# Three feed-forwards of a two-block network, cut by quarters, with 512-column matmuls over both parts of the activation

## The reference

```
u = rms_norm(h, norm_mlp[l])                                       # (256, 1024)
h = h + jnp.square(jax.nn.relu(u @ w_up[l])) @ w_down[l]           # w_up (1024, 4096), w_down (4096, 1024)
```

## Time and profile before

| | |
|---|---|
| median of 3 runs | 1058.03 us (1057.1 to 1058.78) |
| span of the profiled execution, first to last instruction | 1055.0 us |
| mean granted TensorE clock | 0.998 |
| busy: PE, PEld, DVE, ACT, POOL | 98%, 96%, 68%, 51%, 3% |
| moved by DMA | 167.01 MB, mean 158 GB/s |

### The profile page before, as it was taken

One profiled execution on the slowest core, in us unless ns is written; L12 is line 12 of the kernel. 1 busy time (PEld: TensorE's weight loads), 2 busy tenths in 40 slices (PEclk: granted clock), 3 DMA queues, 4 the chain that ended last, 5 costly groups with the idle time before them and its releaser, 6 DMA issues.

```text
span 1055.0 us, 21161 instructions
## 1 busy us (share of the span) xinstructions
PE 1038.3 (98%) x8984; PEld 1008.7 (96%) x8984; DVE 715.8 (68%) x1007; ACT 536.1 (51%) x639; POOL 32.6 (3%) x39
## 2 busy tenths in 40 slices
PE   7999999999999999999999999999999999999997
PEld 7999999999997899999999999999898999999997
DVE  6989665455567787666565567899978666555454
ACT  7847553434446464355445346897543255443431
POOL 0004000000000000000000000042000000000000
PEclk9999999999999999999999999999999999999999
DMA  9722475546744646565555553424100257555511
GB/s 293 222 81 82 160 262 177 194 166 203 275 157 141 219 160 204 159 186 211 186 172 184 182 191 120 140 73 152 58 2 2 64 179 253 183 189 171 196 40 40
DMA packets 119057, 167.01 MB, mean 158 GB/s; under 512 B 5840, under 2 KB 99664, under 8 KB 118608
## 3 DMA queue, kind: packets, MB, share of 16 engines
q1 hardware_dynamic: 117808, 165.92, 47.9%
q10 hardware_dynamic: 1184, 0.17, 0.1%
HBM read 165.03 MB, written 1.05 MB: 157 GB/s over the span
## 4 chain that ended last, share of the span: by engine, by line
PE 84%; DVE 10%; ACT 2%; issue 2%; SPq 1%; DMA 1%; DVEq 0%; ACTq 0%
PE banks L2084 25%; PE banks L2086 25%; PE banks L2085 24%; DVE sb_w_low L1237 2%; DVE sb_arena L1917 1%; DVE sb_state L1914 1%; DMA sb_raw<-in_w_in 1%; PE banks L2668 1%; PE banks L2535 1%; SPq L539 1%; PE banks L2779 0%; DVE sb_arena L1405 0%; DVE sb_state L1402 0%; PE banks L2838 0%; PE banks L2822 0%
## 5 line engine op out<-in xcount | busy, mean ns | idle before, releaser
L1237 DVE TENSOR_TENSOR sb_w_low<-sb_raw,sb_w_high 128x2048 fp32r<-128x2048 f32 x148 | 338.0, 2289 | 242.1 <-ACT sb_w_high L660 242.0
L660 ACT ACTIVATE sb_w_high<-sb_raw 128x2048 fp32r<-128x2048 f32 x148 | 281.8, 1911 | 262.9 <-PE banks L2086 261.7
L2084 PE MATMUL banks<-sb_act_high,sb_w_low 128*128 128x256 f32 x1352 | 386.3, 286 | 1.1 <-DVE sb_arena L1790 0.7
L2086 PE MATMUL banks<-sb_act_high,sb_w_high 128*128 128x256 f32 x1352 | 381.9, 282 | 0.0
L2085 PE MATMUL banks<-sb_act_low,sb_w_high 128*128 128x256 f32 x1352 | 380.0, 281 | 0.0
L2084 PEld LDWEIGHTS banks<-sb_act_high,sb_w_low 128*128 128x128 f32 x1352 | 254.6, 188 | 3.3 <-DVE sb_arena L1790 0.9
L2085 PEld LDWEIGHTS banks<-sb_act_low,sb_w_high 128*128 128x128 f32 x1352 | 255.9, 189 | 0.5 <-issue 0.2
L2084 PE MATMUL banks<-sb_hidden_high,sb_w_low 128*128 128x256 f32 x896 | 253.6, 283 | 0.0
L2086 PEld LDWEIGHTS banks<-sb_act_high,sb_w_high 128*128 128x128 f32 x1352 | 253.4, 187 | 0.0
L2086 PE MATMUL banks<-sb_hidden_high,sb_w_high 128*128 128x256 f32 x896 | 253.4, 283 | 0.0
L2085 PE MATMUL banks<-sb_hidden_low,sb_w_high 128*128 128x256 f32 x896 | 251.9, 281 | 0.0
(11 more groups left out here) (443 smaller groups left out, 1048.6 us busy)
## 6 DMA issues: line engine op xcount, KB each, us to landing
sb_raw<-in_ffn_w SPq DMA_DIRECT2D x64, 1024.0 KB, 5.2
sb_raw<-in_w_up SPq DMA_DIRECT2D x16, 1024.0 KB, 5.4
sb_raw<-in_w_down SPq DMA_DIRECT2D x16, 1024.0 KB, 5.0
sb_raw<-in_sgu_w_in SPq DMA_DIRECT2D x16, 1024.0 KB, 5.3
sb_raw<-in_rwkv_w_rkv SPq DMA_DIRECT2D x12, 1024.0 KB, 5.2
sb_raw<-in_w_in SPq DMA_DIRECT2D x8, 1024.0 KB, 9.6
sb_raw<-in_sgu_w_out SPq DMA_DIRECT2D x8, 1024.0 KB, 4.9
sb_raw<-in_w_out SPq DMA_DIRECT2D x4, 1024.0 KB, 5.1
```

Source lines behind the costliest of these rows:

```text
L660: nc.scalar.activation(whi[s][:], raw[s][:], ACT.Copy).then_inc(hi_done, 1)
L1237: nc.vector.tensor_tensor(wlo[s][:], raw[s][:], f32(whi[s][:]), ALU.subtract).then_inc(lo_done, 1)
L2084: nc.tensor.matmul(dst, l_lo, r_hi, start=start, stop=False, **kw)
L2086: return nc.tensor.matmul(dst, l_hi, r_hi, start=False, stop=stop, **kw)
```

## The change

The feed-forward goes in four quarters of 1024 hidden channels. A quarter is four up units and then four down units, and a down unit now multiplies the quarter's 1024 hidden channels with 256 output channels (`inner` loads, not `outer`). `FFN_ORDER` lists the 32 units. High and low part of an activation tile lie in one buffer, so that one moving operand of 2 x 256 columns has both. `wide` issues two matmuls in place of three: the high weights times both parts, 512 columns over a whole bank, and the low weights times the high part, 256 columns into the bank's second half. The two halves of a bank have to be added, which `add_half` does for the two tiles of a unit by one `tensor_reduce` on DVE, of 2 x 256 x 2 values. Units go round three pairs of banks; PE waits before unit m until unit m-3 is taken. An up unit is then relu-squared by one scalar_tensor_tensor on DVE (max with 0, times itself), copied to the high part by ACT, subtracted by DVE. A down unit is scaled and added to `x` at once, a quarter of the sum at a time. The first two down units of a quarter are interleaved: 6 of 8 k tiles of each, then the last 2 of each. The last unit of a feed-forward uses `split_matmul` as before and is taken by tiles. All loops are unrolled. The low parts of the next stage come after the last full unit has been taken.

```diff
+    act_parts = place("act_parts", 0, [P, 2, KT, T], F32R)
+    act_hi, act_lo = act_parts[:, 0], act_parts[:, 1]
...
+    FFN_ORDER = []
+    for _q in range(4):
+        FFN_ORDER += [("up", i) for i in range(4 * _q, 4 * _q + 4)]
+        FFN_ORDER += [("down", _q, n) for n in range(4)]
+    FFN_BANK = lambda m: 2 * (m % 3)
+    halves_at = lambda b: banks[:, 512 * b:512 * b + 1024].rearrange("p (t h n) -> p t h n", t=2, h=2)
...
 (ACT, mlp)
+            for m in range(len(FFN_ORDER) - 1):
+                if m + 4 < len(FFN_ORDER) or (m + 4 < len(FFN_ORDER) + 2 and u0 + m + 4 < n_units):
+                    high(u0 + m + 4)
+                if FFN_ORDER[m][0] == "up":
+                    hidden_high(m)
...
 (DVE, mlp)
+            def add_half(m, t):
+                dve.wait_ge(w_used, u0 + m + 1)
+                nc.vector.tensor_reduce(t, halves_at(FFN_BANK(m)).rearrange("p t h n -> p t n h"), AX_X, ALU.add)\
+                    .then_inc(unit_taken, 1)
+                dve.wait_ge(unit_taken, 31 * j + m + 1)
+            def up_taken(m):
+                if FFN_ORDER[m][1] or j:
+                    dve.wait_ge(h_sq, 16 * j + FFN_ORDER[m][1])
+                add_half(m, FB.r)
+                nc.vector.scalar_tensor_tensor(FB.h, FB.r, 0.0, FB.r, ALU.max, ALU.mult).then_inc(h_sq, 1)
+            def hidden_low(m):
+                i = FFN_ORDER[m][1]
+                slot = FB.slots[i % 4]
+                dve.wait_ge(h_hi, h0 + i + 1)
+                nc.vector.tensor_tensor(slot[:, 1], FB.h, f32(slot[:, 0]), ALU.subtract).then_inc(h_lo, 1)
+            def down_taken(m):
+                q, n = FFN_ORDER[m][1:]
+                d = down_before(m)
+                t = FB.t[j][d % 2]
+                if d == 14:
+                    dve.wait_ge(x_done, FFN_XO[j] + 1)
+                elif d >= 2:
+                    dve.wait_ge(x_added, 12 * j + min(d - 1, 12))
+                add_half(m, t)
+                chain.add(nc.vector.tensor_tensor(t, t, over(FB.r2[j], 2), ALU.mult))
+                if q:
+                    dve.wait_ge(x_added, 12 * j + 4 * (q - 1) + n + 1)
+                chain.settle()
+                xs = x[:, 2 * n:2 * n + 2, :]
+                nc.vector.tensor_tensor(xs, xs, t, ALU.add).then_inc(x_done if q == 3 else x_added, 1)
+            for m in range(len(FFN_ORDER) - 1):
+                if FFN_ORDER[m][0] == "up":
+                    up_taken(m)
+                else:
+                    down_taken(m)
+                u = u0 + m + 3
+                if m and (m + 3 < len(FFN_ORDER) or (m + 3 < len(FFN_ORDER) + 2 and u < n_units)):
+                    low(u)
+                if FFN_ORDER[m][0] == "up":
+                    hidden_low(m)
+                if m == 3:
+                    token_scale()
...
+            for c in range(3):
+                after_sum(c)
+            t, b = FB.t[j][1], FFN_BANK(len(FFN_ORDER) - 1)
...
+            for i in range(2):
+                if i:
+                    dve.wait_ge(w_used, u0 + len(FFN_ORDER))
+                else:
+                    dve.wait_ge(last_tile, j + 1)
+                chain.add(nc.vector.tensor_tensor(t[:, i, :], tiles_at(b)[:, i, :], FB.r2[j], ALU.mult))
                 chain.settle()
+                nc.vector.tensor_tensor(x[:, 6 + i, :], x[:, 6 + i, :], t[:, i, :], ALU.add)\
+                    .then_inc(x_done if i else x_tile, 1)
+            after_sum(3)
...
 (PE, mlp)
+            def wide(dst, l_hi, l_lo, parts, start, stop):
+                nc.tensor.matmul(two(dst), l_hi, parts, start=start, stop=False, skip_group_check=True)
+                return nc.tensor.matmul(dst[:, T:2 * T], l_lo, parts[:, 0, :], start=False, stop=stop,
+                                        skip_group_check=True)
+            def begin(m):
+                q = (u0 + m) % RING
+                pe.wait_ge(lo_done, u0 + m + 1)
+                if m >= 3:
+                    pe.wait_ge(unit_taken, 31 * j + m - 2)
+                return (w[q][:, :].rearrange("p (k n) -> p k n", k=KT) for w in (whi, wlo))
...
+            for m0 in range(0, len(FFN_ORDER), 8):
+                for m in range(m0, m0 + 4):
+                    up(m)
+                if m0 == 0:
                     pe.wait_ge(sq_folded, j + 1)
                     nc.tensor.matmul(bank[6][:, 0:T], ones, FB.ss[j], start=True, stop=True).then_inc(ss_done, 1)
+                down(m0 + 4, range(6))
+                down(m0 + 5, range(6))
+                down(m0 + 4, range(6, KT))
+                down(m0 + 5, range(6, KT))
+                down(m0 + 6)
+                if m0 + 7 < len(FFN_ORDER) - 1:
+                    down(m0 + 7)
+                else:
+                    down_last(m0 + 7)
```

More of the change, by code:

```diff
@@ L499, in mlp @@
                 sp.wait_ge(tail_ps, ps_at(3, "Y"))
[L500 to L517, removed]
+            for m in range(2, len(FFN_ORDER)):
+                if m == 6 and j == 1 and on["rwkv"]:
+                    load_lora_first()
+                if m == len(FFN_ORDER) - 2:
+                    after_loop()
+                kind, *at = FFN_ORDER[m]
+                if kind == "up":
+                    inner(u0 + m, up, at[0])
+                else:
+                    q, n = at
+                    inner(u0 + m, down[:, 8 * q:8 * q + 8, :], n)
         def load_sgu():
@@ L857, in mlp @@
             high(u0 + 3)
[L859 to L900, removed]
-                        n = i - 2
-                        act.wait_ge(la_scaled, n + 1)
-                        nc.scalar.activation(la_hi[n][:], RW.la_sc[n], ACT.Copy).then_inc(la_hi_done, 1)
-            else:
-                with act.Fori(1, FCH - 2) as i:
-                    body(i)
@@ L1565, in body, with token_scale @@
-            def body(i, last):
-                hidden(i)
-                low(u0 + 6, i)
-                low(u0 + 7, i)
-                if not last:
-                    low(u0 + 8, i)
-                    low(u0 + 9, i)
-            if j == 1 and on["rwkv"]:
-                for i in range(FCH - 2):
-                    body(i, False)
-                    if i in (1, 2):
-                        scale_lora(i - 1)
-                    elif i in (3, 4):
-                        n = i - 3
+            def token_scale():
+                dve.wait_ge(ss_done, SS[("ffn1", "ffn2", "ffn3")[j]] + 1)
+                chain.add(nc.vector.tensor_scalar(FB.r2[j], bank[6][:, 0:T], 1.0 / D, EPS, ALU.mult, ALU.add))
+                chain.settle()
+                chain.add(nc.vector.reciprocal(FB.r2[j], FB.r2[j]))
@@ L1592, in mlp @@
-            chain.settle()
-            for c in range(4 if j < 2 else 3):
-                accumulated(FFN_ACC[j], c, u0 + 4 * FCH)
-                t = FB.t[j][c % 2]
-                if c >= 2:
-                    dve.wait_ge(x_done, FFN_XO[j] + c - 1)
-                chain.add(nc.vector.tensor_tensor(t, two(bank[2 + c][:]), over(FB.r2[j], 2), ALU.mult))
-                chain.settle()
-                xs = x[:, 2 * c:2 * c + 2, :]
-                nc.vector.tensor_tensor(xs, xs, t, ALU.add).then_inc(x_done, 1)
-                after_sum(c)
@@ new lines, in down @@
+            def down(m, ks=range(KT)):
+                q = FFN_ORDER[m][1]
+                h, l = begin(m)
+                pe.wait_ge(h_lo, h0 + 4 * q + ks[-1] // 2 + 1)
+                for t in range(2):
+                    for k in ks:
+                        cs = slice(t * P, t * P + P)
+                        ins = wide(bank[FFN_BANK(m) + t], h[:, k, cs], l[:, k, cs], hidden_of(q, k),
+                                   start=k == 0, stop=k == KT - 1)
+                if ks[-1] == KT - 1:
+                    ins.then_inc(w_used, 1)
```

133 lines of the change are left out of this document (54 added, 79 removed).

## The result

The changed kernel takes 1067.15 us in the median (1064.91 to 1068.02, 4 runs), the kernel before beside it 1057.57 (1056.92 to 1058.78): a ratio of 1.0087, 95% interval 1.0073 to 1.0101. The prediction had 1060.0 with a range of 1050 to 1070: slower, as it said, but by 9.6 us instead of 2.0. The profiled execution took 1064.91 us with a span of 1063.1, 8.1 over the 1055.0 of before; the other three have spans of 1064.7 to 1066.2, so it is the fast end. Two of the three show a lower mean clock (0.993 and 0.992 where it has 0.996), which is the likely reason for them; the third has the same 0.996 and is still 1.6 us longer, which stays open.

The account below looks back on a forecast made before the run. PE's matmul pace was taken to bound the feed-forwards. Feed-forwards and tails summed as -1.3 + 2.4 - 1.3 + 3.0 + 0.2 = +3.0 us; with 353.6 ns groups +2.0 was forecast, 1060.0 us, own range 1056 to 1064, full range 1050 to 1070.

Parts of the forecast that it names:

- What bounds the kernel, and the pace before: In the feed-forwards only PE's own pace sets the time: 120.0 ns per 256-column matmul, 360 ns per group.
- The group: PE's matmuls per (tile, k) in wide units: 354.4 ns instead of 360, 8.4 us in all.
- The reduce: VectorE's new sum of two bank halves per unit: 1024 values at one per cycle, 1.22 us.
- The rival that VectorE bounds the feed-forward by a slow reduce: Reduce below one value per cycle, deciding from 1.5 us; at 2.12 us +55, 1113 us; chance 0.12.
- the rival's mark: Sign of the slow-reduce case: PE would stand still at each quarter's start.
- Starts: Before each feed-forward's first down unit PE waits for VectorE's slot 2: gaps of 1.4, 1.4 and 3 us.
- Steady quarters: At later quarters' first down units VectorE has slot 2 ready 0.8 us earlier than needed: no stall.
- The loads: Weight loads stay 1 MB per unit, issued some 12 us before they are needed: no effect.
- The second feed-forward: Said to have the same distances as the first: 1.4 us start stall, no later stalls, end 1.3 us earlier.
- The gating start: After the first feed-forward PE's next matmul waits for VectorE's remaining work and a low part: +2.4 us.
- The RWKV start: After the second feed-forward VectorE's chain ends 6.0 us after PE's end instead of 2.97: +3.0 us.
- the second row costing as a matmul does: Rival: the wide operand's second row costs a full matmul, group 360 ns, PE gives nothing; +10, 1068 us, chance 0.10.

Follow-up runs that it names:

- e8: The kernel with start, tails and lora steps all reordered (1046.74 us), each wide matmul issued as two of 256 columns; median 1057.69 us, 1.0006 of the kernel before.
- e4: The changed kernel with each 512-column matmul issued as two of 256 columns against the same weights; median 1071.85 us.
- e2: The changed kernel with the fold of squares moved behind hidden slot 2 and PE's sum of squares behind the first down part; median 1059.79 us.
- e1: The changed kernel with VectorE's scaling and splitting of the RWKV layer's first weights moved to units 11, 19, 27, where VectorE waits; median 1060.86 us.
- e6: The changed kernel with six unused fp32 matmuls put into each of the two longest PE pauses; median 1062.89 us.
- e3: The changed kernel with the tails of the first two feed-forwards reordered: later-wanted low parts behind the last residual adds, first normalised ones ahead of unit 30; median 1064.95 us.
- e7: The changed kernel with one more VectorE addition of 232 elements, its result unused, behind each reduce; one execution, span 1076.1 us.
- e9: e3 with the low parts of the RWKV layer's second and third weight unit moved behind the sums of the small products; median 1060.56 us.

## Why the prediction was right in sign and wrong in size

**What bounds the kernel, and the pace before.** Right. e8 shows it from the other side: with three matmuls per group the new order, freed of its stalls, runs as the kernel before does.

**The group.** Too slow by 4.4 ns: 350 instead of 354.4 (by 3.6 against the 353.6 behind the forecast). I added the pace of three wide matmuls in a row to that of three narrow ones, but in turns the narrow one costs 117 and the wide one 233. It is 1.15 us per quarter, some 13 us in all where I had 8.4; the bounds (341.4 to 360) held, and a second row in the moving operand costs nothing: 233 ns, where 512 columns of one row take 234.4. Whether the 10 ns under 360 belong to the weight load or to the matmul that is gone isn't shown, since e4 and e8 put both back. The 325 ns by the gap that the Trainium skill ("TensorE: Matmul & The Clock Gate", Back-to-back issue gap) gives for a matmul by itself are further off than the sum of the rows was.

**The reduce.** Right: 1219 ns for 1.22, 93 times within 14 ns, although it changes half a bank at every element. The rival that VectorE bounds the feed-forward by a slow reduce is out. The Trainium skill ("SBUF — State Buffer", the box on cachelines) speaks of matmuls that non-contiguous PSUM patterns slow down; this read by VectorE was not slowed. But the rival's mark, PE standing still at the start of quarters, did appear, in the second feed-forward, from another cause.

**Starts.** 1.4, 1.4 and about 3 us were forecast; the waits are 1.40, 1.43 and 2.90 us, each ended by VectorE's low part of slot 2, and e2 takes away 1.6, 1.7 and 1.8 by moving the 2.3 us fold that I had named as their first term. The second of them, and the wait before the first gating product:

```profile
486.32 0.47 PE L2437 MATMUL banks<-sb_hidden_slots,sb_w_high 128*128 128x512 f32 x1 [1.43 <-DVE sb_hidden_slot L1550]
```

```profile
312.35 0.47 PE L2074 MATMUL banks<-sb_w_high,sb_act_parts 128*128 128x512 f32 x1 [2.53 <-DVE sb_act_parts L1504]
```

What the starts cost was summed up wrongly in words: "3 are lost as stalls at the starts" is 6.0 by the prediction's own terms (8.4 that PE gives, -2.4 left over the three feed-forwards). Measured it is 6.7: with the better pace PE comes earlier and waits longer.

**Steady quarters.** Right for two feed-forwards: no stall by VectorE, with 1.1 us of margin instead of 0.8. The loads, put at nothing, cost 0.18 us at unit 42.

**The second feed-forward.** This is the step that failed: "The second feed-forward has the same distances." It has not. VectorE's list there holds 9 us more, four steps of 2.2 to 2.4 us, which the loop of before hid in an engine that was half idle. I had worked out a margin of 0.8 us and did not ask what else stands in that list, although the change moves exactly these lines. e1 gives it back: 7.1 us, of which 1.3 to 1.4 are clock (e6).

**Tails.** The gating start was 2.4, measured 2.75. The RWKV start was 3.0 and is 4.8: the last x add is some 6 us behind PE's end as forecast, and the sum of squares waits until 7.7 us behind it instead of 4.5, so the mechanism holds, and this wait is 3.2 us longer, where 3.0 were forecast. The rest is in the windows behind the pause of 2.78 us that ends at 658.62:

```profile
660.00:661.00 1.00, 1.00 (x6) 0.91 (x5) 0.00 (x0) 0.86 (x3) 0.00 (x0) 0.50 1.10 350
661.00:662.00 1.00, 1.00 (x7) 1.00 (x6) 0.56 (x3) 0.98 (x2) 0.00 (x0) 0.50 1.09 346
```

The matmuls come every 213 ns instead of 120 and the records of the sums every 427 instead of 216. From the first of the four sums to the eleventh matmul behind them it is 3.73 us, where before has 2.15: 1.6 us, and e6, which kept the clock there, is shorter by just that. That a pause costs more than its length was nowhere in the sum, and it is the likely reason for most of the 2.2 us by which the median lies above the profiled run.

**The sum, by the terms as they are:** 0.2 - 2.5 + 2.75 + 4.4 + 4.8 - 1.1 - 0.4 = 8.15, and 8.1 was measured. Without the lora steps (7.1) and the clock at the RWKV start (1.6) it would be -0.6. That is the working's +3.0, less 3.9 in the feed-forwards (the pace gives 4.6 more than the 8.4, longer waits at the starts take 0.7 of it back), plus 0.3 and 0.2 at the tails, less 0.2 in the rest.

**What was luck.** The measured time lies outside the range that the forecast had for itself, 1056 to 1064, and inside the 1050 to 1070 that was drawn to take in the rivals. None of the rivals is what happened. The one that comes nearest in time, the second row costing as a matmul does (1068), is ruled out by the 350 ns in the trace and by e4, which issues the rows as two matmuls and takes 1071.85. Two errors of opposite sign, a pace that was better than assumed and two costs that were not in the sum, left a slowdown of the forecast sign; with e1's edit alone, the change is still slower than before (1.0031, 1.0019 to 1.0042).

## What to carry to other kernels

When a change fills an engine that was half idle, list everything that engine does in each copy of the stage and not only in the one you worked out: the work that the idle time hid comes out at full price, less the margin. Give the order of a nearly full engine the same care as the bound engine's: here it was worth 20 us (1067.15 to 1046.74) with not one instruction less, the clock behind the pauses included. Price a pause of TensorE as its length plus what the lower clock may cost behind it: here 1.3 to 2.7 us, behind some of the pauses of 1.95 to 4.5 us.

## What was not expected of the hardware

- A 512-column and a 256-column fp32r matmul in turns take 350 ns (233 + 117), less than 234.4 + 120.0 when each is among its own kind. Why is open.
- The clock behind a pause of PE is not set by the pause's length alone. From start to start of two matmuls: 1.8 us never (ten times), 1.95 yes (e3), 2.36 yes and no (e7, at 152.2 and 492.1), 2.8 no at 312.35 and yes at 658.62 in one and the same execution, 3.28 no in the changed kernel and in e9 but yes in e1 and e3, 3.4 yes in three and no in e2. What decides is open. Its price was 1.3 to 2.7 us. Six matmuls in the pause kept the clock in the one execution of e6 that has a profile.
- VectorE's next independent instruction runs in the gap between a reduce and the instruction that waits for it: 0.39 us of work cost 0.19.
